# The second feed-forward matrix by seven block products in place of eight, in a float32 encoder step

## Chip, core and metric

The kernel runs on one core of a Trainium2 chip. The metric is the device time of one execution in microseconds (us), from the first to the last instruction's work; less is better. Beside the times of plain runs there is one profiled execution, whose trace gives every instruction's start and duration. TensorE multiplies, VectorE and ScalarE work elementwise, GpSimd (POOL) does little here, SyncE (SP) issues the loads of weights.

## What is computed

One layer of an encoder for 512 prompt tokens and 64 sample tokens (T = 576), width 1024, all in float32. The part that is touched is the last third, the feed-forward with its residual, and the final norm:

```python
hn = rmsnorm(x, norm2_g[l]) * (1 + sc2) + sh2
x = x + gt2 * (jnp.square(jax.nn.relu(hn @ w_ff1[l])) @ w_ff2[l])
...
y = rmsnorm(x, final_norm_g) * (1 + scf) + shf
```

w_ff1 is 1024 x 4096 and w_ff2 4096 x 1024. Everything before (norms, projections, a convolution, a gated delta rule) is the same in both kernels.

## The kernel before

**Tiles.** x and all activations lie with features on partitions: 8 feature tiles of 128 by 576 tokens. A weight tile is 8 blocks of 128 x 128 (all 1024 inputs for 128 outputs, 512 KB). The program has 160 such tiles in a row, N_FF = 96 is the first of the feed-forward's 64. Every float32 product is made of three products of a rounded high part and a low part: w_hi by f_hi, w_hi by f_lo, w_lo by f_hi (line 617). With 8 blocks, three products and two halves of 288 tokens (HALF), a tile is 48 matmuls of 288 columns into two PSUM banks; tiles alternate between two pairs of banks of gp.

**How a tile is made ready.** SP loads tile n + 4 into one of four places of w_raw once tile n is split (load, line 309). ScalarE rounds it (w_hi, two places, w_split, line 1096), VectorE subtracts (w_lo, lo_split, line 1496). Both do tile n + 2 right behind the copy of tile n out of PSUM (evac, line 1250), so that a tile is ready well ahead.

**Feed-forward.** The hidden 4096 features go in four quarters, q = 0 to 3, of 1024. ff1(q) makes 8 tiles of relu(.)^2 (VectorE line 1945, f_hi line 1418, f_lo line 1948) in one of two buffers. ff2(q) takes those 8 as inputs and adds the result of each output tile, times the gate, onto xT (add_residual, line 1953). The order is ff1(0), then ff1(q + 1) and ff2(q) for q = 0, 1, 2, then ff2(3). TensorE goes from one to the next without a wait for f, since a whole ff1 lies between.

**The end.** In ff2(3) each finished tile of xT is squared, scaled and transposed to token order between the products (to_tokens, line 1021). The last tile is made in two parts of 384 and 192 tokens (last_products, line 1057), and the sum of squares of the first part, its root and the first rows of y are made while TensorE works on the second. The orders on all engines are written out by hand; counters (semaphores such as tile_done, w_lo_done, bank_free) tie them together. Each engine works through its own list in order, so an instruction that waits holds up all behind it.

## Time and profile before

| | us |
|---|---|
| median of 3 runs | 1243.01 |
| lowest, highest | 1242.7, 1244.49 |
| span of the profiled execution, first to last instruction | 1241.9 |
| TensorE busy (PE) | 1220.0, 98% |
| VectorE busy (DVE) | 659.3, 53% |
| ScalarE busy (ACT) | 441.4, 36% |
| feed-forward, first product to end of the span | 813.8 to 1241.9 |
| last ff2 (q = 3), start | 1175.45 |

The profile gives busy time by engine, groups of instructions by line, the chain that ended last, and the timeline of any stretch. In its rows PE is TensorE, DVE VectorE, ACT ScalarE; a trailing q means the engine's sequencer, such as SPq for DMA issues. Durations of matmuls overlap, so the pace of TensorE is read from starts.

### The profile page before, as it was taken

What the parts mean: (1) busy time and instruction counts of PE and PEld (TensorE: products, weight loads), DVE (VectorE), ACT (ScalarE), POOL (GpSimd) and SP (SyncE); (2) the same over time, 40 slices, a digit from 0 to 9 for tenths busy, and PEclk for the clock granted to TensorE, in tenths of its full rate; (3) what the DMA queues carried; (4) which work ended last, traced back from release to release, by engine and by line L of the source; (5) the groups of instructions that cost most, each with busy time, mean ns of one, the idle gap of its engine ahead of it and who ended that gap; (6) DMA issues with size and microseconds to landing.
All of it is one profiled execution on the core that took longest, in us unless ns stands there. A gap on an engine that the chain in (4) does not pass through costs nothing.

```text
span 1241.9 us, 27254 instructions
## 1 busy us (share of the span) xinstructions
PE 1220.0 (98%) x11471; PEld 1167.6 (94%) x11471; DVE 659.3 (53%) x920; ACT 441.4 (36%) x792; POOL 121.0 (10%) x281
## 2 busy tenths in 40 slices
PE   6999999999999999999999999999999999999997
PEld 3899999999999999989999999979999999999997
DVE  5675666445464454535968984463443343343334
ACT  4584443122232221315243333363332332232254
POOL 4011112102012021021100001000200000000000
PEclk8999999999999999999999999999999999999999
DMA  9732323212222122235855557413422222322212
GB/s 330 237 82 72 86 71 93 65 49 70 78 69 61 53 69 57 58 89 181 245 169 145 168 205 303 121 52 85 136 77 77 84 84 85 85 85 75 81 52 77
DMA packets 181566, 135.44 MB, mean 109 GB/s; under 512 B 4554, under 2 KB 168876, under 8 KB 180184
## 3 DMA queue, kind: packets, MB, share of 16 engines
q1 hardware_dynamic: 174228, 105.36, 29.3%
q0 software_dynamic: 6976, 28.48, 6.8%
q8 instruction: 80, 1.31, 0.4%
q14 instruction: 22, 0.18, 0.0%
q10 hardware_dynamic: 260, 0.10, 0.0%
HBM read 128.02 MB, written 5.90 MB: 108 GB/s over the span
## 4 chain that ended last, share of the span: by engine, by line
PE 95%; DVE 2%; DMA 1%; ACT 1%; SPq 1%; issue 0%; POOL 0%; DVEq 0%; ACTq 0%
PE gp L617 81%; PE dp L847 2%; PE dp L857 1%; DMA ada_w<-in_ada_w 1%; PE gp L643 1%; PE dp L914 1%; PE dp L880 1%; PE dp L907 1%; PE dp L899 1%; PE dp L859 1%; PE dp L886 1%; PE dp L817 1%; PE dp L661 0%; SPq L317 0%; PE dp L889 0%
## 5 line engine op out<-in xcount | busy, mean ns | idle before, releaser
L617 PE MATMUL gp<-a_hi,w_hi 128*128 128x288 f32 x1888 | 414.8, 301 | 1.6 <-DVE w_lo L1496 1.6
L617 PE MATMUL gp<-a_hi,w_lo 128*128 128x288 f32 x1888 | 404.1, 296 | 0.0
L617 PE MATMUL gp<-a_lo,w_hi 128*128 128x288 f32 x1888 | 403.7, 295 | 0.0
L617 PEld LDWEIGHTS gp<-a_hi,w_hi 128*128 128x128 f32 x1888 | 302.1, 189 | 13.8 <-issue 6.1
L617 PEld LDWEIGHTS gp<-a_hi,w_lo 128*128 128x128 f32 x1888 | 303.9, 189 | 0.0
L617 PEld LDWEIGHTS gp<-a_lo,w_hi 128*128 128x128 f32 x1888 | 303.7, 189 | 0.0
L1496 DVE TENSOR_TENSOR w_lo<-w_raw,w_hi 128x1024 fp32r<-128x1024 f32 x160 | 198.0, 1238 | 110.2 <-ACT w_hi L1096 109.3
L1250 ACT ACTIVATE xp<-gp 128x576 f32<-128x576 f32 x113 | 73.7, 652 | 455.2 <-PE gp L617 435.1
L1096 ACT ACTIVATE w_hi<-w_raw 128x1024 fp32r<-128x1024 f32 x160 | 168.7, 1054 | 0.0
L617 PE MATMUL gp<-f_hi,w_hi 128*128 128x288 f32 x496 | 106.7, 297 | 0.0
L617 PE MATMUL gp<-f_hi,w_lo 128*128 128x288 f32 x496 | 106.3, 296 | 0.0
L617 PE MATMUL gp<-f_lo,w_hi 128*128 128x288 f32 x496 | 106.2, 296 | 0.0
L1953 DVE SCALAR_TENSOR_TENSOR xT<-xp,mod,xT 128x512 f32 (+3 forms) x62 | 29.4, 516 | 123.4 <-ACT xp L1250 123.4
L1945 DVE SCALAR_TENSOR_TENSOR acc<-xp 128x576 f32<-128x576 f32 x32 | 24.3, 758 | 109.8 <-ACT xp L1250 109.8
L617 PEld LDWEIGHTS gp<-f_hi,w_lo 128*128 128x128 f32 x496 | 79.9, 189 | 0.0
L617 PEld LDWEIGHTS gp<-f_lo,w_hi 128*128 128x128 f32 x496 | 79.9, 189 | 0.0
L617 PEld LDWEIGHTS gp<-f_hi,w_hi 128*128 128x128 f32 x496 | 79.8, 189 | 0.0
L1857 DVE SCALAR_TENSOR_TENSOR ada_sum<-ada_half,c_act,ada_sum 128x1024 f32<-128x1024 f32 x56 | 68.7, 1280 | 0.0
L1629 DVE SCALAR_TENSOR_TENSOR acc<-xp,vecs,acc 128x579 f32<-128x579 f32 x72 | 59.2, 822 | 7.1 <-DVE acc L1627 1.2
L1715 DVE TENSOR_TENSOR mm<-mm,dp 128x256 f32<-128x256 f32 (+1 forms) x45 | 15.9, 391 | 74.6 <-PE dp L859 74.6
L518 POOL TENSOR_TENSOR nb<-at,lvl 128x512 f32<-128x512 f32 (+1 forms) x30 | 35.5, 1189 | 73.7 <-PE dp L847 51.9
L1260 ACT ACTIVATE p<-dp 128x256 f32<-128x256 f32 (+1 forms) x25 | 9.2, 367 | 91.0 <-PE dp L847 91.0
(322 smaller groups left out, 1206.5 us busy)
## 6 DMA issues: line engine op xcount, KB each, us to landing
w_raw<-in_w_in SPq DMA_DIRECT2D x72, 512.0 KB, 3.8
w_raw<-in_w_ff SPq DMA_DIRECT2D x64, 512.0 KB, 4.0
ada_half<-in_ada_w POOLq DMA_DIRECT2D x32, 512.0 KB, 4.6
ada_w<-in_ada_w SPq DMA_DIRECT2D x16, 512.0 KB, 9.8
w_raw<-in_w_a_out SPq DMA_DIRECT2D x8, 512.0 KB, 4.2
w_raw<-in_w_b_out SPq DMA_DIRECT2D x8, 512.0 KB, 3.9
w_raw<-in_w_o SPq DMA_DIRECT2D x8, 512.0 KB, 6.2
fin_vu<-in_final_ada_w POOLq DMA_DIRECT2D x4, 1024.0 KB, 18.0
```

What stands on the lines that cost most here:

```text
L518: pool.tensor_tensor(nb[:, l % 2, 0:n].rearrange("p c h i -> p (c h) i"), at_[:, 0:n].rearrange("p c h i -> p (c h) i"), m, ALU.mult).then ...
L617: last = T_.matmul(gp[:, 2 * b + h, 0:HALF], wp[:, b, k, :], ap[:, k, h * HALF:(h + 1) * HALF], start=(k == 0 and wp is w_hi and ap is hi) ...
L643: last = T_.matmul(gp[:, 2 * b + h, 0:HALF], wp[:, b, k, :], ap[:, k, h * HALF:(h + 1) * HALF], start=(k == 0 and wp is w_hi and ap is hi) ...
L847: last = T_.matmul(cols(B3[o, at * CH:(at + 1) * CH], l, 0), nb[b, l % 2, e, hp, :], cols(mm[b, 0, e, hp, :], l, 0), start=True, stop=True)
L1096: AC(w_hi[:, j % 2, :, :], w_raw[:, j, :, :], ACT.Copy).then_inc(S["w_hi_done"], 1)
L1250: AC(halves(out), bank(b), func, scale=scale).then_inc(S["bank_free"], 1)
L1496: TT(w_lo[:, j % 2, :, :], w_raw[:, j, :, :], w_hi[:, j % 2, :, :].bitcast(F32), ALU.subtract)\
L1629: ins = STT(acc[:, b, 0:W], xp[:, b, tap:tap + W], cw[:, tap, ds(n, 1)], acc[:, b, 0:W], ALU.mult, ALU.add)
L1715: last = TT(m, m, cols(dp[:, 2 + t, 0:n * HP * CH], l, t), ALU.add)
L1857: STT(out, w, c_act[:, k, g:g + 1], out, ALU.mult, ALU.add).then_inc(S["ada_added"], 1)
L1945: STT(acc[:, b, 0:T], xp[:, b, 0:T], 0.0, xp[:, b, 0:T], ALU.max, ALU.mult).then_inc(S["tmp_free"], 1)
L1953: last = STT(xT[:, t, c], xp[:, b, c], mod_c(t, g), xT[:, t, c], ALU.mult, ALU.add)
```

## The change

The second matrix is applied in pairs: two output tiles (256 features) by eight input tiles, taken as a 2 x 2 arrangement of weight blocks (even and odd input tiles e, first and second output tile) against a 2 x 2 arrangement of activations (even and odd tiles, first and second half of the tokens). Such a 2 x 2 product is formed from seven block products in place of eight, with sums of blocks on both sides. A block product is four 128 x 128 blocks by 288 tokens, three times: 12 matmuls. There are 16 such pairs (q = 0 to 3, m = 0 to 3).

- **Weights.** The seven are called w11, w12, w22 (plain blocks) and s1 to s4 (sums). SP loads per pair one whole tile, the block w21 twice (once for s1, once into w_s3) and w22. VectorE forms s1 = w21 + w22, s2 = s1 + w11, s4 = s2 + w12 in place, and s3 = w21 + w11 (add_weights, line 2219). Each block product has its own w_hi (hi_of, line 1627) and w_lo (lo_of, line 2204) of 512 columns, in rings of four half places.
- **Activations.** For two hidden tiles f has seven halves (f_hi, f_lo): three as they are, four as differences (f_sum, lines 2232 to 2240), 1152 columns in two of the steps. There are five such sets.
- **Order.** In place of ff1 and ff2 there are "up" pairs (two tiles of w_ff1, 96 matmuls) and "down" pairs. Four down pairs stand in a run; before the run of q = 0, 1, 2 goes the first up pair of q + 1, behind it the other three. The run of q = 3 follows its last up pair at once.
- **Results.** PSUM banks hold running sums from which others are taken: ScalarE copies a bank to keep1, keep2 or keep5 (keep, lines 1656 and 1661), VectorE subtracts that from another bank (the mixes, lines 2267, 2272, 2277; each counts mixed_in) and adds the result to xT (lines 2254, 2290). The last product of a pair is read from PSUM. The product s1 of the next pair stands between s2 and s3 and is written to the bank that the first mix (keep1) reads; it waits for it.
- **The end.** xT's last two feature tiles are finished together. Squares are summed on VectorE over pairs of tiles; last_products and its two parts are gone.
- The loops over tiles are written out. In the diff ITEMS is the list of all products in order, issued(k) gives those whose place in the ring of halves comes free with product k.

```diff
+def ff_plan():
+    pairs = [("up", 0, u) for u in range(4)]
+    for q in range(4):
+        if q < 3:
+            pairs.append(("up", q + 1, 0))
+        pairs += [("down", q, m) for m in range(4)]
+        if q < 3:
+            pairs += [("up", q + 1, u) for u in range(1, 4)]
+    items, at = [], 0
+    for p, (kind, q, i) in enumerate(pairs):
+        if kind == "up":
+            names = [(p, "a", 2), (p, "b", 2)]
+        else:
+            names = [(p, "s1", 1)] if i == 0 else []
+            names += [(p, "w11", 1), (p, "w12", 1), (p, "s2", 1)]
+            names += [(p + 1, "s1", 1)] if i < 3 else []
+            names += [(p, "s3", 1), (p, "s4", 1), (p, "w22", 1)]
+        for name in names:
+            items.append(name + (at,))
+            at += name[2]
+    return pairs, items
...
+        def load_first(p):
...
+                sp.wait_ge(S["w_lo_done"], split_items(p - 2, "a" if PAIRS[p - 2][0] == "up" else "s4"))
+            sp.dma_start(w_raw[:, 2 * (p % 2), :, :], w_block(p, "w1")).then_inc(first_full[p % 2], 16)
+        def load_second(p):
...
+            sp.wait_ge(S["w_lo_done"], split_items(p - 2, "b" if PAIRS[p - 2][0] == "up" else "s4"))
+            sp.dma_start(raw_block(p, "s1"), w_block(p, "w21")).then_inc(sum_full[p % 2], 16)
+            if PAIRS[p - 2][0] == "down":
+                sp.wait_ge(S["w_lo_done"], split_items(p - 2, "w22"))
+            sp.dma_start(raw_block(p, "w22"), w_block(p, "w22")).then_inc(second_full[p % 2], 16)
+        def load_s3(p):
+            if p > DOWN[0]:
+                sp.wait_ge(S["w_lo_done"], split_items(DOWN[DOWN.index(p) - 1], "s3"))
+            sp.dma_start(w_s3[:, :, :], w_block(p, "w21")).then_inc(s3_full, 16)
+        for p in range(1, len(PAIRS)):
+            load_first(p)
+            if PAIRS[p - 1][0] == "down":
+                load_s3(p - 1)
+            load_second(p)
+        load_s3(len(PAIRS) - 1)
...
+        def down(p, name, units=range(4)):
+            q, i = PAIRS[p][1:]
+            d = downs(p)
+            z, y, x = i % 2, 1 - i % 2, 2 + i % 2
+            bank, blk, opens = {"s1": (z, 3, True), "w11": (x, 0, True), "w12": (y, 2, True), "s2": (x, 4, False),
+                                "s3": (x, 5, False), "s4": (z, 1, False), "w22": (x, 6, False)}[name]
+            if 0 in units:
+                pe.wait_ge(S["w_lo_done"], split_items(p, name))
+                if name == "s1" and i == 0:
+                    pe.wait_ge(S["bank_free"], N_FF + 2 * ups(p) - 2 + 3)
+                elif name == "s1":
+                    pe.wait_ge(S["mixed_in"], 3 * (d - 1) + 1)
+                elif name == "w11" and i < 2:
+                    pe.wait_ge(S["bank_free"], N_FF + 2 * ups(p) - 1 + 3)
+                elif name == "w11":
+                    pe.wait_ge(S["x_new"], 4 * (d - 1))
+                elif name == "w12" and i:
+                    pe.wait_ge(S["mixed_in"], 3 * (d - 1) + 3)
+                elif name == "s2":
+                    pe.wait_ge(S["kept_out"], kept(p, "keep1"))
+                elif name == "s3":
+                    pe.wait_ge(S["kept_out"], kept(p, "keep2"))
+                elif name == "s4":
+                    pe.wait_ge(S["kept_out"], kept(p, "keep5"))
+                elif name == "w22":
+                    pe.wait_ge(S["mixed_in"], 3 * d + 2)
+            for u in units:
+                if i == 0:
+                    pe.wait_ge(S["f_split"], 4 * q + u + 1)
+                f = (4 * q + u) % FW
+                s0 = (END[p, name] - 1) % 4
+                for wp, ap in ((w_hi, f_hi), (w_hi, f_lo), (w_lo, f_hi)):
+                    last = T_.matmul(gp[:, bank, 0:HALF], wp[:, s0 // 2, 4 * (s0 % 2) + u, :], ap[f][:, blk, :],
+                                     start=(opens and u == 0 and wp is w_hi and ap is f_hi), stop=(u == 3 and wp is w_lo),
+                                     skip_group_check=True)
+            if 3 in units:
+                last.then_inc(S["slot_done"], 1)
...
+        def hi_of(k):
+            p, name, width, at = ITEMS[k]
...
+                act.wait_ge(S["slot_done"], at + width - 4)
+            if name in ("a", "w11", "w12"):
+                act.wait_ge(first_full[p % 2], ADA_IN + 16 * loads_before(p, "first"))
+            elif name in ("b", "w22"):
+                act.wait_ge(second_full[p % 2], ADA_IN + 16 * loads_before(p, "second"))
+            else:
+                act.wait_ge(S["w_summed"], summed(p, name))
+            AC(slots(w_hi, k), raw_block(p, name), ACT.Copy).then_inc(S["w_hi_done"], 1)
+        def keep(p, name):
+            i, d = PAIRS[p][2], downs(p)
+            z, x = i % 2, 2 + i % 2
+            if name == "keep5":
+                act.wait_ge(S["slot_done"], END[p, "s1"])
+                if d >= 2:
+                    act.wait_ge(S["x_new"], 4 * (d - 2) + 2)
+                AC(keep5[d % 2][:, :], gp[:, z, 0:HALF], ACT.Copy).then_inc(S["kept_out"], 1)
+            else:
+                act.wait_ge(S["slot_done"], END[p, "w11" if name == "keep1" else "s2"])
+                if d:
+                    act.wait_ge(S["x_new"], 4 * (d - 1) + (1 if name == "keep1" else 3))
+                AC((keep1 if name == "keep1" else keep2)[:, :], gp[:, x, 0:HALF], ACT.Copy).then_inc(S["kept_out"], 1)
...
-        def ff2(q, n0):
-            with dve.Fori(0, 2) as i:
-                for j in range(4):
-                    n, b, t = n0 + 4 * i + j, j % 2, 4 * i + j
-                    dve.wait_ge(S["bank_free"], n + 1 + 2)
-                    add_residual(t, b).then_inc(S["tmp_free"], 1)
-                    lo_split(n + 2, (j + 2) % 4)
+        def lo_of(k):
+            p, name = ITEMS[k][:2]
+            dve.wait_ge(S["w_hi_done"], N_FF + k + 1)
+            TT(slots(w_lo, k), raw_block(p, name), slots(w_hi, k).bitcast(F32), ALU.subtract).then_inc(S["w_lo_done"], 1)
+        def add_weights(k):
+            p, name = ITEMS[k][:2]
+            other = {"s1": "w22", "s2": "w11", "s3": "w11", "s4": "w12"}[name]
+            if name == "s1":
+                dve.wait_ge(sum_full[p % 2], ADA_IN + 16 * loads_before(p, "sum"))
+                dve.wait_ge(second_full[p % 2], ADA_IN + 16 * loads_before(p, "second"))
+            else:
+                dve.wait_ge(first_full[p % 2], ADA_IN + 16 * loads_before(p, "first"))
+            if name == "s3":
+                dve.wait_ge(s3_full, ADA_IN + 16 * loads_before(p, "s3"))
+            elif name != "s1":
+                dve.wait_ge(S["w_lo_done"], split_items(p, "s1" if name == "s2" else "s2"))
+            TT(raw_block(p, name), raw_block(p, name), raw_block(p, other), ALU.add).then_inc(S["w_summed"], 1)
+        def up_step(p, tile, ks):
+            n, j = N_FF + 2 * ups(p) + tile, ups(p)
+            hi, lo = f_hi[j % FW], f_lo[j % FW]
+            even, odd = [(acc[:, e, HALF:T], acc[:, e, 0:HALF]) for e in range(2)]
+            dve.wait_ge(S["bank_free"], n + 1 + 2)
+            STT(acc[:, tile, 0:T], xp[:, tile, 0:T], 0.0, xp[:, tile, 0:T], ALU.max, ALU.mult).then_inc(S["tmp_free"], 1)
+            for k in ks:
+                lo_of(k)
+            dve.wait_ge(S["tmp_free"], n - N_WA + 3)
+            if tile == 0:
+                TT(f_sum[:, 0, :], even[0], even[1], ALU.subtract).then_inc(S["f_summed"], 1)
+                dve.wait_ge(S["f_hi_done"], 3 * j + 1)
+                STT(lo[:, 0, :], acc[:, 0, HALF:T], -1.0, hi[:, 0, :].bitcast(F32), ALU.mult, ALU.subtract)
+                return
+            dve.wait_ge(S["f_summed"], 2 * j + 1)
+            ch.note(TT(f_sum[:, 1, :], odd[1], f_sum[:, 0, :], ALU.add))
+            TT(f_sum[:, 2, :], even[1], odd[1], ALU.subtract)
+            ch.wait()
+            TT(f_sum[:, 3, :], odd[0], f_sum[:, 1, :], ALU.subtract).then_inc(S["f_summed"], 1)
+            dve.wait_ge(S["f_hi_done"], 3 * j + 2)
+            TT(lo[:, 1:3, :], acc[:, 1, 0:T].rearrange("p (h c) -> p h c", h=2), hi[:, 1:3, :].bitcast(F32), ALU.subtract)
+            dve.wait_ge(S["f_hi_done"], 3 * j + 3)
+            TT(lo[:, 3:7, :], f_sum[:, :, :], hi[:, 3:7, :].bitcast(F32), ALU.subtract).then_inc(S["f_split"], 1)
...
+        def down_step(p, name, ks):
+            q, i = PAIRS[p][1:]
+            d, t = downs(p), 2 * i
+            z, y, x = i % 2, 1 - i % 2, 2 + i % 2
+            if name == "w12":
+                dve.wait_ge(S["slot_done"], END[p, "w12"])
+                dve.wait_ge(S["kept_out"], kept(p, "keep1"))
+                TT(keep1[:, :], gp[:, y, 0:HALF], keep1[:, :], ALU.subtract).then_inc(S["mixed_in"], 1)
+                after = (t, LATE, keep1, HALF, 4 * d)
+            elif name == "s3":
+                dve.wait_ge(S["slot_done"], END[p, "s3"])
+                dve.wait_ge(S["kept_out"], kept(p, "keep5"))
+                TT(keep5[d % 2][:, :], gp[:, x, 0:HALF], keep5[d % 2][:, :], ALU.subtract).then_inc(S["mixed_in"], 1)
+                after = (t + 1, EARLY, keep5[d % 2], 0, 4 * d + 1)
+            elif name == "s4":
+                dve.wait_ge(S["slot_done"], END[p, "s4"])
+                dve.wait_ge(S["kept_out"], kept(p, "keep2"))
+                TT(keep2[:, :], gp[:, z, 0:HALF], keep2[:, :], ALU.subtract).then_inc(S["mixed_in"], 1)
+                after = (t, EARLY, keep2, 0, 4 * d + 2)
+            for k in ks:
+                lo_of(k)
+            if name in ("w12", "s3", "s4"):
+                dve.wait_ge(S["mixed_in"], 3 * d + {"w12": 1, "s3": 2, "s4": 3}[name])
+                onto_x(*after).then_inc(S["x_new"], 1)
+            elif name == "w22":
+                dve.wait_ge(S["slot_done"], END[p, "w22"])
+                j = 4 * d + 3
+                if j >= 16:
+                    dve.wait_ge(S["x_new"], j - 15)
+                for g, c in LATE:
+                    last = STT(xT[:, t + 1, c], gp[:, x, c.start - HALF:c.stop - HALF], mod[:, 2, t + 1 + KT:t + 2 + KT, g],
+                               xT[:, t + 1, c], ALU.mult, ALU.add)
+                last.then_inc(S["x_new"], 1)
...
+                down_step(p, name, issued(k))
+                if q == 3 and i and name == "s2":
+                    sum_squares(i - 1)
+            for m in (issued(k + 1) if k + 1 < len(ITEMS) else ()):
+                if ITEMS[m][1][0] == "s":
+                    add_weights(m)
```

**How the orders move.** The first place is VectorE in the middle of a run of second-matrix work. Before, for each output tile, from the start of a loop over ff2's tiles:

```order
L1953 ISA [waits bank_free]
L1953 ISA
L1953 SCALAR_TENSOR_TENSOR xT<-xp,mod,xT 128x512
L1953 ISA
L1953 SCALAR_TENSOR_TENSOR xT<-xp,mod,xT 128x64
L1496 TENSOR_TENSOR w_lo<-w_raw,w_hi 128x1024 [waits w_hi_done]
L1963 REGISTER_ALU
```

Now, in a pair in the middle of a run, from the sum s2 to the first mix (keep_143 is keep1, keep_144 keep2, w_s_142 is w_s3):

```order
L2219 TENSOR_TENSOR w_raw<-w_raw 128x512 [waits w_lo_done,ada_full1]
L2277 TENSOR_TENSOR keep_144<-gp,keep_144 128x288 [waits kept_out,slot_done]
L2204 TENSOR_TENSOR w_lo<-w_raw,w_hi 128x512 [waits w_hi_done]
L2254 SCALAR_TENSOR_TENSOR xT<-keep_144,mod,xT 128x288 [waits x_new,mixed_in]
L2219 TENSOR_TENSOR w_raw<-w_raw 128x512 [waits ada_full2,ada_full4]
L2204 TENSOR_TENSOR w_lo<-w_raw,w_hi 128x512 [waits w_hi_done]
L2290 SCALAR_TENSOR_TENSOR xT<-gp,mod,xT 128x224 [waits x_new,slot_done]
L2290 SCALAR_TENSOR_TENSOR xT<-gp,mod,xT 128x64
L2219 TENSOR_TENSOR w_s_142<-w_s_142,w_raw 128x512 [waits ada_full6,ada_full1]
L2204 TENSOR_TENSOR w_lo<-w_s_142,w_hi 128x512 [waits w_hi_done]
L2219 TENSOR_TENSOR w_raw<-w_raw 128x512 [waits w_lo_done,ada_full1]
L2267 TENSOR_TENSOR keep_143<-gp,keep_143 128x288 [waits kept_out,slot_done]
```

One w_lo of 1024 columns and a residual per tile have become sums, mixes, w_lo of 512 columns and residuals in turn.

The second place is VectorE where the first matrix's tile gives way to the second's. Before, the last tile of ff1(1) and the small work on the last norm's scale behind it:

```order
L1944 REGISTER_ALU
L1945 SCALAR_TENSOR_TENSOR acc<-xp 128x576 [waits bank_free]
L1496 TENSOR_TENSOR w_lo<-w_raw,w_hi 128x1024 [waits w_hi_done]
L1947 REGISTER_ALU
L1948 ISA [waits f_hi_done]
L1948 TENSOR_TENSOR f_lo<-acc,f_hi 128x576
L1941 REGISTER_ALU
L1941 COMPARE_AND_BRANCH
L1529 TENSOR_TENSOR mod<-dp,vecs 128x32 [waits ada_t]
L1535 TENSOR_SCALAR scales<-mod 128x16 [waits dve_own]
L1536 TENSOR_TENSOR scales<-scales,vecs 128x16 [waits dve_own]
```

Now, the end of the last up pair and the first steps of the run:

```order
L2204 TENSOR_TENSOR w_lo<-w_raw,w_hi 128x512 [waits w_hi_done] x2
L2237 TENSOR_TENSOR f_sum<-acc,f_sum 128x288 [waits f_summed,tmp_free]
L2238 TENSOR_TENSOR f_sum<-acc 128x288
L2240 TENSOR_TENSOR f_sum<-acc,f_sum 128x288 [waits dve_own]
L2242 TENSOR_TENSOR f_lo_138<-acc,f_hi_133 128x576 [waits f_hi_done]
L2244 TENSOR_TENSOR f_lo_138<-f_sum,f_hi_133 128x1152 [waits f_hi_done]
L2219 TENSOR_TENSOR w_raw<-w_raw 128x512 [waits ada_full2,ada_full4]
L2204 TENSOR_TENSOR w_lo<-w_raw,w_hi 128x512 [waits w_hi_done]
L2219 TENSOR_TENSOR w_s_142<-w_s_142,w_raw 128x512 [waits ada_full6,ada_full1]
L2204 TENSOR_TENSOR w_lo<-w_s_142,w_hi 128x512 [waits w_hi_done]
L2219 TENSOR_TENSOR w_raw<-w_raw 128x512 [waits w_lo_done,ada_full1]
L2267 TENSOR_TENSOR keep_143<-gp,keep_143 128x288 [waits kept_out,slot_done]
```

The low parts of f stand ahead of sum s1 of the next pair, and three sums ahead of the first mix.

The third place is ScalarE in the same kind of work. Before, from the start of the loop over ff2's tiles:

```order
L1249 REGISTER_ALU [waits tile_done]
L1250 ACTIVATE xp<-gp 128x576 [waits tmp_free]
L1095 ISA
L1096 ACTIVATE w_hi<-w_raw 128x1024 [waits w_raw_full2]
L1247 REGISTER_ALU
```

Now, from w_hi of s2 and s1 on through one pair (keep_1_146 is keep5):

```order
L1627 ACTIVATE w_hi<-w_raw 128x512 [waits w_summed,slot_done] x2
L1661 ACTIVATE keep_143<-gp 128x288 [waits x_new,slot_done]
L1627 ACTIVATE w_hi<-w_s_142 128x512 [waits w_summed,slot_done]
L1627 ACTIVATE w_hi<-w_raw 128x512 [waits w_summed,slot_done]
L1661 ACTIVATE keep_144<-gp 128x288 [waits x_new,slot_done]
L1627 ACTIVATE w_hi<-w_raw 128x512 [waits ada_full3,slot_done]
L1656 ACTIVATE keep_1_146<-gp 128x288 [waits x_new,slot_done]
L1627 ACTIVATE w_hi<-w_raw 128x512 [waits ada_full0,slot_done] x2
L1627 ACTIVATE w_hi<-w_raw 128x512 [waits w_summed,slot_done]
L1627 ACTIVATE w_hi<-w_s_142 128x512 [waits w_summed,slot_done]
```

Copies to keep1, keep2 and keep5 stand between roundings, some of which wait for VectorE's sums (w_summed).

## Rows read from the trace of the kernel before

**Rows 1.** The page: busy time by engine, and the chain by engine

```profile
PE 1220.0 (98%) x11471; PEld 1167.6 (94%) x11471; DVE 659.3 (53%) x920; ACT 441.4 (36%) x792; POOL 121.0 (10%) x281
...
PE 95%; DVE 2%; DMA 1%; ACT 1%; SPq 1%; issue 0%; POOL 0%; DVEq 0%; ACTq 0%
```

**Rows 2.** Chain that ended last, 1130 to 1242: start, us, what

```profile
1129.91 45.33 PE gp L617 x340
...
1175.45 12.78 PE gp L617 x96
1188.24 0.44 PE dp L1021 x4
```

**Rows 3.** Stretches: length, PE, PEld, DVE, ACT, POOL busy, clock, DMA share, GB/s

```profile
1087.00:1141.00 54.00, 54.00 (x407) 54.00 (x406) 22.17 (x27) 17.81 (x24) 0.00 (x0) 1.00 0.27 78
...
1175.00:1223.00 48.00, 48.00 (x368) 47.99 (x367) 18.92 (x26) 24.03 (x45) 2.20 (x4) 1.00 0.14 38
```

**Rows 4.** Timeline at a tile's end in ff2(2): start, us, engine, instruction

```profile
1130.28 0.42 PE L617 MATMUL gp<-f_hi,w_hi 128*128 128x288 f32 x2
...
1130.56 0.65 ACT L1250 ACTIVATE xp<-gp 128x576 f32<-128x576 f32 x1 [4.21 <-PE gp L617]
...
1131.11 1.05 ACT L1096 ACTIVATE w_hi<-w_raw 128x1024 fp32r<-128x1024 f32 x1
...
1132.35 1.22 DVE L1496 TENSOR_TENSOR w_lo<-w_raw,w_hi 128x1024 fp32r<-128x1024 f32 x1
```

**Rows 5.** Timeline in ff1(1)

```profile
881.08 1.05 ACT L1096 ACTIVATE w_hi<-w_raw 128x1024 fp32r<-128x1024 f32 x1
...
882.17 1.23 DVE L1496 TENSOR_TENSOR w_lo<-w_raw,w_hi 128x1024 fp32r<-128x1024 f32 x1 [0.19 <-ACT w_hi L1096]
883.31 0.75 DVE L1948 TENSOR_TENSOR f_lo<-acc,f_hi 128x576 f32 x1
```

**Rows 6.** Groups on VectorE by form: busy us, mean ns, idle before

```profile
L1945 DVE SCALAR_TENSOR_TENSOR acc<-xp 128x576 f32<-128x576 f32 x32 | 24.3, 758 | 109.8 <-ACT xp L1250 109.8
...
L1953 DVE SCALAR_TENSOR_TENSOR xT<-xp,mod,xT 128x512 f32 x24 | 18.0, 752 | 102.2 <-ACT xp L1250 102.2
...
L1953 DVE SCALAR_TENSOR_TENSOR xT<-xp,mod,xT 128x64 f32 x24 | 6.7, 279 | 0.0
...
L1725 DVE TENSOR_TENSOR kbe<-by_chunk,eg 128x512 f32<-128x512 f32 x9 | 6.1, 683 | 0.0
...
L1600 DVE TENSOR_TENSOR row<-dp,row 64x288 f32<-64x288 f32 x1 | 0.4, 443 | 0.0
```

**Rows 7.** Groups on ScalarE by form: busy us, mean ns, idle before

```profile
L1207 ACT ACTIVATE xp<-gp 128x288 f32<-128x288 f32 x24 | 9.8, 410 | 77.3 <-PE gp L617 77.3
...
L1163 ACT ACTIVATE ab_both<-ab_raw 128x512 fp32r<-128x512 f32 x1 | 0.6, 630 | 2.7 <-POOL ab_raw L469 2.7
```

**Rows 8.** SP's issues (ns), and DMA of 750 to 813: packets, MB, share; us to landing

```profile
L309 SPq DMA_DIRECT2D w_raw<-in_w_ff x64: 372/373/1251, 776.9 to 1193.1; - x64
...
q1 hardware_dynamic: 9939, 5.01, 29.2%
...
w_raw<-in_w_ff SPq DMA_DIRECT2D x6, 512.0 KB, 4.0
```

**Rows 9.** Last matmuls with w_lo (start range), and VectorE's timeline at the end

```profile
L1057 PE MATMUL gp<-f_hi,w_lo x16: 272/306/342, 1223.7 to 1232.7; 128*128 128x384 f32 x8, 128*128 128x192 f32 x8
...
1231.12 1.15 DVE L1986 SCALAR_TENSOR_TENSOR z_tok<-z_tok,rstd,shift 128x896 f32<-128x896 f32 x1 [1.86 <-ACT rstd L1468]
...
1237.30 1.27 DVE L2006 SCALAR_TENSOR_TENSOR z_smp<-z_smp,rstd,shift 64x1024 f32<-64x1024 f32 x1
```

**Rows 10.** TensorE early: timeline, and stretches with PE busy, clock, DMA share, GB/s

```profile
22.74 1.89 PE L661 MATMUL dp<-ada_w,c_act 128*2 128x512 f32 x8 [1.87 <-DMA ada_w<-in_ada_w]
...
22.00:23.00 1.00, 0.26 (x4) 0.58 1.23 243
32.00:33.00 1.00, 1.00 (x9) 0.80 1.06 389
```

470 lines of the change are left out of this document (285 added, 185 removed).

## The prediction

> **What bounds the kernel now.** I read the engines' shares and the chain first: TensorE is busy 98% of the span and carries 95% of the chain that ended last [rows 1]. The pieces of the chain in the feed-forward show it without a gap: 340 matmuls of 288 columns in 45.33 us, 96 in 12.78 us, so 0.1333 us each and 6.40 us for a tile of 48 [rows 2]. The table of stretches gives VectorE's load there: 22.2 us of 54 and, in the last ff2, 18.9 of 48, with the clock at full [rows 3]. So today a matmul taken away is time taken away, and VectorE and ScalarE have room on average. Average room isn't what decides here. The timeline shows how one tile is handed on: the next tile's first matmul starts at 1130.28, ScalarE's copy of the finished bank at 1130.56 (0.28 later), w_hi ends at 1132.16 and VectorE's w_lo starts at 1132.35 [rows 4]. In a tile that has a second step the handover from ScalarE to VectorE is only 0.04 (882.13 to 882.17) [rows 5]. A weight tile is made two tiles ahead, so all of it hides behind 6.40 us. After the change the unit is a product of 12 matmuls, 1.60 us, and the hand-overs come seven to a pair.
>
> **What goes.** 16 pairs of output tiles take 84 matmuls in place of 96: 192 x 0.1333 = 25.6 us of TensorE, all on the chain. The loops' registers go too (0.25 of idle VectorE time before x, hidden).
>
> **What comes, in rows' prices.** VectorE with two tensors: 512 columns 0.68, 576 columns 0.75, 1024 columns 1.22, 288 columns out of PSUM 0.44, a square of 576 0.76 [rows 4 to 6]. Back to back the next starts 0.09 before the end (882.17 to 883.31 for 1.23 long [rows 5]), so steps of 0.60, 0.66, 1.14 and 0.37. The residual step on 288 columns: 0.75 for 512 and 0.28 for 64 [rows 6] give 0.52, a step of 0.43; in two parts 0.56. ScalarE: 512 columns 0.63, 288 out of PSUM 0.41 [rows 7]. A pair then asks VectorE for 7 w_lo and 4 sums (11 x 0.60), 3 mixes (1.1), residuals (2 x 0.43 + 2 x 0.56): 9.7 us of work in the 11.2 us that the pair's 84 matmuls take. That would still fit; the order does not let it run through. Sums s1 and s3 are followed at once, on the same in-order queue, by the w_lo of that very sum, which needs ScalarE's w_hi of it. Sum starts at 0, w_hi at 0.72, w_lo at 1.39: 0.79 us of idle VectorE each; behind sum s2 a mix fills half of it and 0.42 stays.
>
> **The wait that the change adds.** The product s1 of the next pair is written to the bank from which keep1 is mixed, so TensorE waits there for VectorE's mix (line 2267, semaphore mixed_in), which stands at the end of a long stretch of VectorE's queue. I walk one pair in the middle of a run, from the start of s1 at 0. s3 ends at 3.20, seen at 3.48: mix of keep5 to 3.85. w_lo of w12 starts at 4.15 (its w_hi could start only at 3.48), to 4.75; residual to 5.18; sum s2 to 5.78; mix of keep2 to 6.15; w_lo of s2 not before 6.57, to 7.17; residual 7.60; sum s1 starts 7.60, its w_lo 8.99 to 9.59; residual in two parts to 10.14; sum s3 starts 10.14, its w_lo 11.53 to 12.13; sum s4 to 12.73; mix of keep1 12.73 to 13.18; TensorE starts the next s1 at 13.24. A pair thus takes 13.24 us; its matmuls take 11.2 and before it took 12.80. The point from which this decides: from "s3 seen" to "mix done" the queue takes 9.70 us, and it may take 7.66 (11.2 less 3.20, 0.28 and 0.06).
>
> **A whole run of four pairs** (q = 0 to 2), from the end of the last up tile. VectorE first finishes that tile: copy out to 0.93, square 0.96 to 1.64, two w_lo to 2.84, three differences to 3.92, low parts to 4.59, and the 1152-wide one, after ScalarE's copy of 1.15 (its prices for 512 and 1024 columns carried on), to 6.52. Only then sum s1 (w_lo to 8.51), sum s3 (w_lo to 10.50), sum s4 to 11.10, mix to 11.55. TensorE has 6.4 us of work by then and starts s1 of the second pair at 11.6: 5.2 us idle. It also waits for keep1 in between, since ScalarE has w_hi of s1 queued ahead of that copy (s2 starts at 8.2 for 4.8). Two full cycles follow, 26.5. Then s1, s3, s4, w22 are 6.4, and the last pair has no s1 between s2 and s3, so s3 waits for keep2, queued behind two w_hi: 1.2 idle, 10.8 in all. Sum 11.6 + 26.5 + 6.4 + 10.8 = 55.3 against 8 x 6.40 = 51.2: **+4.1 a run, +12.3 for three**. The 6.4 us of matmuls saved in a run come back as 10.5 of waiting. The up tiles between runs ask VectorE for 7.5 us per 12.8 (two w_lo 2.3, two squares 1.4, four differences 1.5, low parts 2.4): nothing changes there.
>
> **The last run** (q = 3) follows straight on up tiles whose f it needs, +0.4. Five additions of squares (0.66 each, about half of them in the waiting queue), ScalarE's squares, scalings and z copies ahead of w_hi and keep copies, and 30 transposes at 0.11 [rows 2] make its two full cycles about 14.3 and its end 20.3: 12.0 + 28.6 + 20.3 = 60.9. Behind it, both parts of the square sums wait for the last product, where now the first y row starts at 1231.12, ahead of the last matmul with w_lo at 1232.7 [rows 9]. From it 1.4 us of sums and roots to the first y, 6.1 for the y rows, 3.3 from the last y to the end as now [rows 9]: I take 10.8. 71.7 against 1241.9 - 1175.45 = 66.5 [rows 2]: **+5.2**.
>
> **Loads.** SP now issues four loads a pair (1.25 MB for 1.0), each 0.37 us to issue [rows 8]. They leave together once s4 is split, at 0.9 of the walk. 5.01 MB took 29.2% of 63 us, 272 GB/s, and a lone 512 KB load lands after 4.0, so 2.1 is fixed [rows 8]. Then 1.25 MB land by 0.9 + 2.1 + 4.8 = 7.8, and sum s1 wants the last of them at 7.60. I take 0; 1 us a pair is the upper bound, at most 7 in all. Below zero is excluded: a load can't make the queue shorter.
>
> **Sum.** 1241.9 + 12.3 + 5.2 = 1259.4 in the profiled execution. The median of the runs lies 1.1 above its span, so **1260.5**, +1.4%. The steps' prices are good to some 3%: eight waiting cycles of 13.2 give 3 us, four run starts 1 each.
>
> A page is weighed here. The trace has the next VectorE instruction start 0.09 before the end of the one ahead [rows 5]. The Trainium skill, "VectorE: DVE Perf Modes", section "The DRAIN you can't avoid", says that the next one doesn't start until the pipe is empty. By that each of some ten back-to-back steps of a cycle would cost 0.09 more, about 9 us over the kernel, and the sum would be near 1269. The trace disagrees for this kernel's instructions, so the row is used; 1269 lies within the forecast's own range.
>
> **Rivals.**
> *VectorE keeps up (faster).* If the sums ran early enough, or w_hi were there when w_lo asks, the mix would be done before s2 ends and only 192 matmuls would count: 1243.0 - 25.6 + 1.5 for the tail = 1219; with the run starts' 5.2 left over four times, 1240. It speaks for it that VectorE's work, 9.7, is under 11.2; against it that its idle 0.79, 0.79 and 0.42 a pair follow from the order, and that s3, whose end starts the walk, can't be earlier. It would need 2 us less in the queue of each pair. 0.13.
> *No change.* The same, half way: a queue 0.5 us shorter in each of eight cycles and starts 1.5 shorter give 1250; to come within 0.2% it takes half as much again, and the stretch of such prices is narrow. 0.03.
> *The clock falls (slower still).* The granted clock fell to half (1.2 GHz) at 22 us, in a stretch in which TensorE waited for loads, the last time for 1.87 us, and was back ten us later [rows 10]. At each run start the change leaves TensorE idle for 5.2 of 6.8 us. If it falls there, the two products that the queue waits for (s1 and s3) take 3.2 each: up to 3.2 a run, 13 in all, 1273. With late loads beside it, 1280. No other stretch of this trace has such a gap with dense matmuls behind it. 0.16.
> The Trainium skill, "TensorE: Matmul & The Clock Gate", section "HAM oscillation — how this bites in real kernels", says that waits which break up the matmuls put the array back to half rate each time. By that rule the time would be this rival's upper end; the trace has one fall behind such waits, and here no run shows it yet in dense matmuls.
> *It doesn't do what it says.* TensorE's new order holds 12 matmuls a product and seven products a pair, so this is out.
>
> **Chances and range.** The forecast, 1248 to 1273, has 0.68; beyond it to 1278 lies half of the clock and load case. That leaves the faster rival and the far end of the slow one outside, some 2 in 10. The range is 1248 to 1278. About 0.2% is what a measurement of this kernel can tell from no change. Faster 0.13, same 0.03, slower 0.84.
>
> **What would show it.** Right: TensorE's busy time some 25 us lower in a longer span; idle time of TensorE put down to VectorE's mixes (line 2267), twelve times, three of them in each run, near 5 us at the starts and 2 us after; starts of s1 about 13.2 us apart; VectorE idle 0.8 us before the w_lo of sums, put down to ScalarE. Wrong: s1 starts 11.2 apart and no wait for mixes; loads named as releaser of the sums; half clock in the runs.

## The result, and the profile after

The changed kernel takes **1274.2 us** (median of 4 executions, 1273.19 to 1275.0), the kernel before 1243.45 beside it (4 executions, 1242.7 to 1244.49): a ratio of 1.0247, 95% interval 1.0232 to 1.0261. It is 30.8 us slower; I had forecast 17.5. The profiled execution has a span of 1271.5 for 1241.9. In what follows a run is the four down pairs of one q, and a cycle is the time from the first matmul of one pair's product s1 to that of the next.

The page of the kernel after: busy time by engine, the chain by engine, and the two groups of the new products and roundings that answer to [rows 1] and [rows 6]:

```profile
PE 1208.5 (95%) x11304; PEld 1149.6 (90%) x11304; DVE 797.9 (63%) x1222; ACT 481.7 (38%) x894; POOL 123.0 (10%) x283
...
PE 81%; DVE 7%; ACT 4%; issue 4%; SPq 2%; DMA 2%; DVEq 0%; POOL 0%; ACTq 0%
...
L1210 PE MATMUL gp<-f_hi,w_hi 128*128 128x288 f32 x448 | 138.3, 309 | 39.9 <-DVE keep L2267 19.6
...
L2204 DVE TENSOR_TENSOR w_lo<-w_raw,w_hi 128x512 fp32r<-128x512 f32 (+1 forms) x126 | 102.4, 818 | 42.7 <-ACT w_hi L1627 42.5
```

TensorE's chain has gone from 95% to 81% of the span: the time is in waits. What TensorE waited for from 820 to 1272, and VectorE in one cycle from s1 to s1 (905.47 to 919.11):

```profile
PE gp L1210 <- DVE keep L2267: 19.6, 12, 2.2
PE gp L1210 <- issue: 10.6, 4, 3.4
PE gp L1210 <- ACT keep L1661: 6.8, 7, 1.3
PE gp L1210 <- DVE f_lo L2244: 2.8, 1, 2.8
...
DVE w_lo L2204 <- ACT w_hi L1627: 3.2, 6, 0.8
```

Twelve waits for the first mix, as forecast, and behind them waits for ScalarE's copies and at the starts of runs ("issue" is a wait whose releaser the profile doesn't name; at 888.35 it ends with ScalarE's copy to keep1). VectorE is idle 3.2 us in a cycle, all of it put down to w_hi. 2.3 of that are holes behind its own sums (0.76, 0.76, 0.39 and 0.39). The other 0.9 stands behind ScalarE, which itself waits for TensorE there: 0.73 behind the copy to keep5, 0.21 behind a rounding.

The starts of the runs are not quite as forecast. The long wait there is the one ahead of s2, 3.3 to 3.4 us in the first three runs, and it ends with the copy to keep1; the wait for the mix that follows is 0.4 to 1.7.

The four runs of down pairs, from the end of the last up tile to the last product, by stretches (us, PE, PEld, DVE, ACT, POOL busy, granted clock, DMA share, GB/s), and then the tail:

```profile
880.09:936.82 56.73, 47.36 (x338) 45.95 (x337) 42.70 (x81) 22.85 (x43) 0.00 (x0) 0.97 0.33 89
986.82:1045.62 58.80, 47.61 (x338) 46.12 (x337) 42.71 (x81) 22.89 (x43) 0.00 (x0) 0.97 0.30 85
1096.89:1158.19 61.30, 49.99 (x338) 48.44 (x337) 42.75 (x81) 22.89 (x43) 0.00 (x0) 0.92 0.30 82
1196.78:1257.38 60.60, 51.93 (x369) 49.27 (x367) 45.67 (x85) 33.77 (x67) 6.39 (x8) 0.97 0.18 50
1257.40:1271.50 14.10, 5.54 (x81) 4.41 (x80) 7.22 (x9) 3.51 (x12) 0.00 (x0) 0.71 0.46 169
```

I had 55.3 for each of the first three, 60.9 and 10.8. VectorE's work is the same 42.7 in the first three though their lengths differ by 4.6: those runs differ in clock and in loads, not in work. In the third the clock is 0.92. A stretch of it:

```profile
1107.00:1108.00 1.00, 0.49 (x3) 0.14 (x1) 1.00 (x2) 0.00 (x0) 0.00 (x0) 0.50 0.00 0
1110.00:1111.00 1.00, 1.00 (x6) 1.00 (x6) 0.74 (x2) 0.00 (x0) 0.00 (x0) 0.50 0.14 42
1115.00:1116.00 1.00, 1.00 (x9) 1.00 (x8) 1.00 (x3) 0.00 (x0) 0.00 (x0) 1.00 0.31 77
```

At 0.50 (1.2 GHz) matmuls start 0.24 us apart, for 0.1333 [rows 2]. It fell 1.1 us after TensorE had resumed from an idle 3.32 and was back at 1113.1.

**One cycle in full**, the timeline of VectorE with the starts of s1 on TensorE (start, us, engine, operation, idle before):

```profile
905.47 0.37 PE L1210 MATMUL gp<-f_hi,w_hi 128*128 128x288 f32 x1 [2.15 <-DVE keep L2267]
...
908.92 0.46 DVE L2272 TENSOR_TENSOR keep<-gp,keep 128x288 f32<-128x288 f32 x1
909.58 0.69 DVE L2204 TENSOR_TENSOR w_lo<-w_raw,w_hi 128x512 fp32r<-128x512 f32 x1 [0.21 <-ACT w_hi L1627]
...
912.07 0.69 DVE L2204 TENSOR_TENSOR w_lo<-w_raw,w_hi 128x512 fp32r<-128x512 f32 x1 [0.39 <-ACT w_hi L1627]
912.68 0.51 DVE L2254 SCALAR_TENSOR_TENSOR xT<-keep,mod,xT 128x288 f32<-128x288 f32 x1
913.26 0.69 DVE L2219 TENSOR_TENSOR w_raw<-w_raw 128x512 f32<-128x512 f32 x1
914.71 0.69 DVE L2204 TENSOR_TENSOR w_lo<-w_raw,w_hi 128x512 fp32r<-128x512 f32 x1 [0.76 <-ACT w_hi L1627]
...
915.87 0.68 DVE L2219 TENSOR_TENSOR w_s<-w_s,w_raw 128x512 f32<-128x512 f32 x1
917.30 0.69 DVE L2204 TENSOR_TENSOR w_lo<-w_s,w_hi 128x512 fp32r<-128x512 f32 x1 [0.76 <-ACT w_hi L1627]
...
918.52 0.45 DVE L2267 TENSOR_TENSOR keep<-gp,keep 128x288 f32<-128x288 f32 x1
919.11 0.37 PE L1210 MATMUL gp<-f_hi,w_hi 128*128 128x288 f32 x1 [2.13 <-DVE keep L2267]
```

The walk of the prediction can be laid beside it, counted from s1: mix of keep5 3.48, here 3.45; w_lo of w12 4.15 and 4.11; w_lo of s2 6.57 and 6.60; sum s1 7.60 and 7.79; sum s3 10.14 and 10.40; first mix 12.73 and 13.05; next s1 13.24 and 13.64. The holes of 0.76 and 0.39 stand where it had 0.79 and 0.42.

### The profile page after: what moved, and what is told of

The parts are those of the page before. It is cut to its first block, busy times and chain, and to the rows that moved or that the text cites. A ratio compares the mean times of both kernels' runs of the same rounds, so it can differ in the third digit from the quotient of the medians.

```text
span 1271.5 us, 26974 instructions
## 1 busy us (share of the span) xinstructions
PE 1208.5 (95%) x11304; PEld 1149.6 (90%) x11304; DVE 797.9 (63%) x1222; ACT 481.7 (38%) x894; POOL 123.0 (10%) x283
## 4 chain that ended last, share of the span: by engine, by line
PE 81%; DVE 7%; ACT 4%; issue 4%; SPq 2%; DMA 2%; DVEq 0%; POOL 0%; ACTq 0%
PE gp L766 48%; PE gp L1172 15%; PE gp L1210 6%; ACT w_hi L1627 3%; PE dp L996 2%; DVE w_raw L2219 2%; SPq L433 1%; PE dp L1006 1%; PE gp L792 1%; DMA ada_w<-in_ada_w 1%; DVE w_s L2219 1%; PE dp L1063 1%; PE dp L1029 1%; DMA w_raw<-in_w_ff 1%; PE dp L1056 1%
## 5 line engine op out<-in xcount | busy, mean ns | idle before, releaser
L766 PEld LDWEIGHTS gp<-a_hi,w_hi 128*128 128x128 f32 x1408 | 224.7, 189 | 11.6 <-issue 6.9
L766 PEld LDWEIGHTS gp<-a_hi,w_lo 128*128 128x128 f32 x1408 | 226.4, 188 | 0.0
L1755 DVE TENSOR_TENSOR w_lo<-w_raw,w_hi 128x1024 fp32r<-128x1024 f32 x98 | 120.2, 1227 | 100.9 <-ACT w_hi L1300 100.1
L1210 PE MATMUL gp<-f_hi,w_hi 128*128 128x288 f32 x448 | 138.3, 309 | 39.9 <-DVE keep L2267 19.6
L1210 PE MATMUL gp<-f_lo,w_hi 128*128 128x288 f32 x448 | 135.7, 303 | 0.0
L1210 PE MATMUL gp<-f_hi,w_lo 128*128 128x288 f32 x448 | 135.7, 303 | 0.0
L2204 DVE TENSOR_TENSOR w_lo<-w_raw,w_hi 128x512 fp32r<-128x512 f32 (+1 forms) x126 | 102.4, 818 | 42.7 <-ACT w_hi L1627 42.5
L1210 PEld LDWEIGHTS gp<-f_hi,w_hi 128*128 128x128 f32 x448 | 87.7, 196 | 45.8 <-issue 36.6
L1627 ACT ACTIVATE w_hi<-w_raw 128x512 fp32r<-128x512 f32 (+1 forms) x126 | 90.4, 729 | 89.8 <-DVE w_raw L2219 64.6
L1454 ACT ACTIVATE xp<-gp 128x576 f32<-128x576 f32 x50 | 32.5, 651 | 191.9 <-PE gp L766 175.3
L1300 ACT ACTIVATE w_hi<-w_raw 128x1024 fp32r<-128x1024 f32 x98 | 103.4, 1056 | 0.5 <-DMA w_raw<-in_w_in 0.5
```

The costliest lines, as they stand in the source:

```text
L766: last = T_.matmul(gp[:, 2 * b + h, 0:HALF], wp[:, b, k, :], ap[:, k, h * HALF:(h + 1) * HALF], start=(k == 0 and wp is w_hi and ap is hi) ...
L1210: last = T_.matmul(gp[:, bank, 0:HALF], wp[:, s0 // 2, 4 * (s0 % 2) + u, :], ap[f][:, blk, :], start=(opens and u == 0 and wp is w_hi and ...
L1300: AC(w_hi[:, j % 2, :, :], w_raw[:, j, :, :], ACT.Copy).then_inc(S["w_hi_done"], 1)
L1454: AC(halves(out), bank(b), func, scale=scale).then_inc(S["bank_free"], 1)
L1627: AC(slots(w_hi, k), raw_block(p, name), ACT.Copy).then_inc(S["w_hi_done"], 1)
L1755: TT(w_lo[:, j % 2, :, :], w_raw[:, j, :, :], w_hi[:, j % 2, :, :].bitcast(F32), ALU.subtract)\
```

## Experiments

The theory at this point: VectorE's queue, with the holes that its sums make, is the pace of a pair, and the run starts are its second half. Rivals: the loads, the clock, ScalarE's order. The table gives for every kernel the median (of four executions; five for "filled holes, loads", two for "no sums") and, from its profiled execution, the length of the four runs of down pairs, from the first product's start to the last one's end; without any wait a run of the first three would be 28 x 1.60 = 44.8.

| kernel | us | ratio to before | run 0, 1, 2, 3 |
|---|---|---|---|
| after | 1274.2 | 1.0247 | 56.6, 58.7, 61.2, 60.7 |
| no sums | 1235.5 | 0.9933 | 47.4, 47.5, 47.4, 54.1 |
| mix moved | 1275.8 | 1.0259 | 57.5, 57.0, 57.2, 64.2 |
| filled waits | 1272.4 | 1.0228 | 57.2, 56.9, 57.9, 61.7 |
| w_s3 loaded last | 1274.5 | 1.0255 | 58.3, 57.7, 58.1, 62.0 |
| filled holes | 1256.4 | 1.0101 | 53.9, 53.0, 54.7, 58.1 |
| mix moved, copies first | 1272.8 | 1.0238 | 57.8, 56.2, 56.7, 63.9 |
| filled holes, early start | 1256.0 | 1.0105 | 49.3, 50.4, 52.1, 58.1 |
| sums on GpSimd | 1263.9 | 1.0169 | 58.5, 52.9, 53.2, 60.9 |
| filled holes, loads | 1248.5 | 1.0038 | 50.8, 50.9, 50.8, 58.2 |
| all of these | 1234.4 | 0.9924 | 45.6, 45.8, 45.7, 59.0 |
| all, copies first | 1238.0 | 0.9953 | 47.4, 47.4, 47.3, 58.8 |

### The sums left out

```diff
                 if ITEMS[m][1][0] == "s":
-                    add_weights(m)
+                    pass
```

ScalarE waits for the loads instead of the sums; the products then use weight blocks that were never added.

> The four weight sums of a pair are left out (ScalarE rounds the raw block as soon as it is loaded); everything else, all 84 matmuls of a pair too, stays. Theory (TensorE waits for the first mix, which stands at the end of a queue of sums, each with a w_lo behind it that waits for ScalarE): without sums the queue from the end of s3 to the mix is 6.9 us by the same prices, under the 7.66 allowed, so the waits for the mix at line 2267 vanish, s1 starts come 11.2 us apart, only a rest of some 2 us at each run start stays: 1228 to 1236 us. Rival (the loss is clock and late loads, or the low parts of f): TensorE still waits, 1255 or more.

Measured: 1235.48, inside the theory's range (ratio 0.9933, 0.9913 to 0.9953). No down product waits for a mix in it, cycles are 11.0 to 11.2, and the first three runs are 47.4 long with the clock at 1.00. The four sums of a pair cost about 39 us, together with the holes behind them and the falls of the clock behind the waits that they make. That is more than the 25.6 that the missing eighth product saves.

### The first mix moved ahead of two sums

In this and the following kernels VectorE's steps are first listed in the order of the kernel after, and then single ones are moved.

```diff
+        for p in DOWN:
+            if PAIRS[p][2] < 3:
+                move(("mix", p, "w12"), before=("add", NTH[p, "s3"]))
```

> Only the place of the first mix (keep1) in VectorE's order is changed: it goes ahead of the sum s3, its w_lo and the sum s4 that stood before it. VectorE's work is the same to the instruction. Theory: the mix is done about when s2 ends, so that wait goes; then VectorE's whole list bounds, 9.7 us of work and 2.8 of waits for ScalarE (s4's w_lo now waits too): 12.5 us a pair in place of 13.6, and run starts of 9.0 in place of 11.75. 4 x 2.7 + 8 x 1.1 = 20 us less: 1254, with the clock's part up to 5 less: 1249 to 1256. Rival (VectorE has simply too much work, order is no matter): 1270 to 1275.

Measured: 1275.79, 1.0259 (1.0241 to 1.0276). My theory said 1249 to 1256, so it was wrong as it stood: TensorE no longer waits for the mix, and the time is the same. TensorE's waits, and VectorE's in the cycle from 1011.33 to 1025.43, which is 14.1 long:

```profile
PE gp L1210 <- ACT keep L1661: 25.6, 19, 2.6
...
DVE w_lo L2204 <- ACT w_hi L1627: 49.8, 91, 1.5
DVE w_raw L2219 <- DMA w_raw<-in_w_ff: 6.8, 6, 1.7
...
1013.88 0.69 DVE L2204 TENSOR_TENSOR w_lo<-w_s,w_hi 128x512 fp32r<-128x512 f32 x1 [0.76 <-ACT w_hi L1627]
1014.49 0.69 DVE L2219 TENSOR_TENSOR w_raw<-w_raw 128x512 f32<-128x512 f32 x1
1015.93 0.69 DVE L2204 TENSOR_TENSOR w_lo<-w_raw,w_hi 128x512 fp32r<-128x512 f32 x1 [0.76 <-ACT w_hi L1627]
...
1023.57 0.69 DVE L2219 TENSOR_TENSOR w_raw<-w_raw 128x512 f32<-128x512 f32 x1 [1.11 <-DMA w_raw<-in_w_ff]
```

The wait has changed its name: TensorE now waits for ScalarE's copies, which stand behind w_hi of s1 and of s4, and these wait for VectorE's sums. VectorE never waits for TensorE in this cycle. Its idle is 0.76 three times, 0.39, and 1.11 for a load, 3.8 in all, and 10.3 of work beside it makes the 14.1. The mix had filled the hole between sum s4 and its w_lo (0.39 was left); moved, it opens that hole to 0.76. Beside the cycle of the kernel after, the 0.9 of idle behind TensorE is gone, and 0.4 of hole and 1.1 of load have come in its place. My theory had counted 9.7 of work, where 10.3 are measured (it took the steps ahead of the holes without their last 0.09), and no load.

The loads are thus part of the answer. Six of VectorE's sums wait for a load here, 6.8 us in all, where two did in the kernel after (2.0). How much the moved mix would have gained with loads in another order was not measured. Two readings are left: VectorE's queue closes on itself whatever TensorE waits for by name (A), or ScalarE's order is the cause (B). Both are tried below.

### Matmuls put into the waits

```diff
+                if q in (1, 2):
+                    for _ in range(24 if name == "s2" and i == 0 else 12 if name == "s1" and i else 6 if name == "s3" and i == 3 else 0):
+                        T_.matmul(dp[:, 0, 0:HALF], a_hi[:, 0, 0:P], a_hi[:, 0, 0:HALF], start=True, stop=True)
                 pe.wait_ge(S["w_lo_done"], split_items(p, name))
```

> Matmuls on a_hi into an unused bank are put into TensorE's waits in the runs of q = 1 and 2: 24 ahead of s2 of the first pair, 12 ahead of every s1 that waits, 6 ahead of s3 of the last pair; their results are used by nothing. Theory that the half clock seen in these two runs costs time by itself: the three falls at 1027, 1106 and 1140 us go, their 1.9 + 1.6 + 1.6 us come back, 1268 to 1271. Rival (slow matmuls hid in waits anyway, the cost was none): 1273 to 1276.

Measured: 1272.36, ratio 1.0228 (1.0211 to 1.0245), between the theory's 1268 to 1271 and the rival's 1273 to 1276. Runs 1 and 2, by stretches:

```profile
989.04:1046.10 57.06, 54.97 (x405) 53.37 (x403) 42.75 (x81) 22.92 (x43) 0.00 (x0) 1.00 0.32 88
1097.35:1155.40 58.05, 54.95 (x405) 53.36 (x403) 42.76 (x81) 22.94 (x43) 0.00 (x0) 1.00 0.31 87
```

The clock is at full in both, and they are 1.8 and 3.3 shorter than in the kernel after: some 5 us for the clock in those two executions. In the median only 1.8 of it can be seen, and the profiled spans differ by 1.3, since runs 0 and 3, which have no such matmuls, are 1.5 longer together, and what lies between and behind the runs is 2.2 longer. Where the clock falls differs from trace to trace: the last run, with the same work in both kernels, has one fall in the kernel after and two here. The clock is a small term; its size is between 1.8 and 5 us.

### The w_s3 block loaded last

```diff
             load_first(p)
+            load_second(p)
             if PAIRS[p - 1][0] == "down":
                 load_s3(p - 1)
-            load_second(p)
```

> SP issues w21 and w22 for a pair's s1 ahead of the block w_s3 for the pair before it, no other change. Theory: the two waits of VectorE for loads (0.7 and 1.3 us, runs of q = 1 and 2) go, since w22 lands 0.25 MB earlier: 1271 to 1273. Rival (load order moves the wait to the sum s3, or noise): 1273 to 1276.

Measured: 1274.5, ratio 1.0255 (1.0238 to 1.0272): no gain that can be told, as the rival said. In the trace cycles without a disturbance are 13.48, and sum s1 stands at 7.62 after s1, where the walk had 7.60. The kernel after has one such cycle, the first of run 1, 13.49 long. In three of its eight cycles (13.61 to 13.64), the shown one among them, the sum starts some 0.15 late, which fits a load that ends just too late; the profile names none. The two late loads that it does name (2.0 us) became others; the waits for loads in this trace:

```profile
DVE w_raw L2219 <- DMA w_raw<-in_w_ff: 1.0, 1, 1.0
DVE w_s L2219 <- DMA w_s<-in_w_ff: 1.0, 2, 0.6
```

### A against B: the holes filled

```diff
+        for p in DOWN:
+            i = PAIRS[p][2]
+            if i < 3:
+                move(("mix", p, "w12"), before=("add", NTH[p, "s3"]))
+                move(("add", NTH[p, "s4"]), after=("add", NTH[p, "s3"]))
+                move(("residual", p, "w12"), after=("lo", NTH[p, "s3"]))
+                move(("residual", p, "s3"), after=("add", NTH[p + 1, "s2"]))
+            if i < 2:
+                move(("residual", p, "w22"), before=("lo", NTH[p + 2, "s1"]))
```

> Steps of VectorE in another order, the same work: for the first three pairs of a run the first mix stands ahead of sum s3 (as in the run with the mix alone moved), sum s4 stands straight behind sum s3 (ahead of w_lo of s3), the residual of w12 behind w_lo of s3, the residual of s3 behind sum s2, the residual of w22 ahead of w_lo of s1. So each gap of 0.76 us between a sum and its own w_lo has a step in it. Theory A, formed after the run with the mix alone moved: VectorE's queue is itself the period of a pair (10.2 us of steps, 3.2 to 3.4 us of waits for ScalarE's w_hi and up to 1.1 for a load in 14.1), and in the run with the mix alone the mix had merely left a gap open that it had filled. With the gaps filled a pair takes 11.2 to 12.8 (12.8 if the load of the next w21 block then ends the wait for sum s1), the kernel 1245 to 1260. Rival B: what holds TensorE is ScalarE's order, copies to keep1 and keep2 that stand behind roundings of sums; that order is not touched here, so no gain over the run with the mix alone: 1270 to 1277.

Measured: 1256.38, ratio 1.0101 (1.0082 to 1.0121), so A's range, 17.8 under the kernel after and 19.4 under the one with the mix alone, with no step removed and ScalarE's order untouched. VectorE's waits for w_hi are 19.4 lower too (30.4 for 49.8), and its waits for loads rise from 6.8 to 11.4. The waits, then the w_lo of a sum and the next sum s1:

```profile
DVE w_lo L2204 <- ACT w_hi L1627: 30.4, 78, 2.2
DVE w_raw L2219 <- DMA w_raw<-in_w_ff: 9.0, 7, 2.2
...
1009.38 0.69 DVE L2204 TENSOR_TENSOR w_lo<-w_s,w_hi 128x512 fp32r<-128x512 f32 x1 [0.16 <-ACT w_hi L1627]
...
1018.26 0.69 DVE L2219 TENSOR_TENSOR w_raw<-w_raw 128x512 f32<-128x512 f32 x1 [2.10 <-DMA w_raw<-in_w_ff]
```

### A against B: ScalarE's copies first

```diff
+            inner = [NTH[r + 1, "s1"] for r in DOWN if PAIRS[r][1] < 3 and PAIRS[r][2] < 3]
+            inner += [NTH[r, "s4"] for r in DOWN if PAIRS[r][1] < 3 and PAIRS[r][2] < 3]
+            if q < 3 and i < 3 and name in ("w11", "s2"):
+                hi_of(NTH[p + 1, "s1"] if name == "w11" else NTH[p, "s4"])
             for m in issued(k):
-                hi_of(m)
+                if m not in inner:
+                    hi_of(m)
```

> The first mix ahead of sum s3, as in the run with the mix alone moved, and on ScalarE, for q < 3 and the first three pairs, the copy to keep1 ahead of w_hi of the next s1 and the copy to keep2 ahead of w_hi of s4. Theory A (VectorE's queue with its gaps is the period): the waits put down to the keep copies (19 of them, 25.6 us) move elsewhere, cycles stay at 13.1 to 14.3, and only the start and end of a run gain some 1 us: 1270 to 1275. Rival B (ScalarE's order holds TensorE): most of the waits for keep go, cycles near 12, the kernel 1250 to 1260.

Measured: 1272.84, ratio 1.0238 (1.0217 to 1.0258), as A said. TensorE's waits for copies go from 25.6 to 11.2 and waits for mixes take their place:

```profile
PE gp L1210 <- DVE keep L2271: 13.5, 14, 2.2
PE gp L1210 <- ACT keep L1661: 11.2, 9, 2.7
PE gp L1210 <- issue: 3.7, 6, 0.9
```

B falls as the main cause. Copies and mixes together are 24.7 for 25.6: for these only the name moved. The waits that the profile calls "issue", mostly at the run starts, did fall, from 10.7 to 3.7 us, and the time by 2.9: ScalarE's order is worth about that much here, not the 20 of rival B.

### The start of a run brought forward

To the filled order, with the w_s3 block loaded last as above:

```diff
+        for p in DOWN:
+            q, i = PAIRS[p][1:]
+            if i == 0:
+                move(("up", p - 1, 1, "differences"), after=("add", NTH[p + 1, "s1"]))
+                if q < 3:
+                    move(("up", p - 1, 1, "low"), after=("residual", p + 3, "s3"))
+                else:
+                    move(("up", p - 1, 1, "low"), after=("up", p - 1, 1, "differences"))
```

ScalarE's wide copy goes behind keep1 of the first pair for q < 3.

> The order of the filled run, and with it: the load of the w_s3 block issued behind the pair's other loads, and at the start of a run the differences of f behind sum s1's place in the queue and, for q < 3, ScalarE's copy of the 1152 columns and VectorE's low part of them put off until the last up tile is needed at the next down run. Theory A: loads no longer end the wait for sum s1, cycles 11.2 to 12, starts 2 us shorter: 1232 to 1246, so faster than the kernel before or equal to it. Rival: if loads or the falling clock bound the filled run, this one is at most 3 us better than it.

Measured: 1255.98, ratio 1.0105 (1.0088 to 1.0122): the theory's 1232 to 1246 is missed and the rival holds, 0.4 better than the filled order. The runs are 9.8 shorter together, but VectorE's waits for loads have grown from 11.4 to 16.7, and TensorE now waits in up tiles:

```profile
DVE w_raw L2226 <- DMA w_raw<-in_w_ff: 8.5, 7, 1.5
DVE w_s L2226 <- DMA w_s<-in_w_ff: 8.2, 3, 3.5
...
PE gp L1172 <- DVE keep L2273: 6.2, 3, 2.1
```

VectorE's sums come 11.9 apart, and the loads are what ends last in that: sum s1 at 1009.95 waits 1.20 for a block that SP issued at 1004.80. And the low part of 1152 columns, put ahead of the last mix of a run, makes the next up tile wait 2.1 us each time. That was my placing.

### The sums on GpSimd

```diff
-                if ITEMS[m][1][0] == "s":
+                if ITEMS[m][1][0] == "s" and PAIRS[ITEMS[m][0]][1] in (0, 3):
                     add_weights(m)
```

For q = 1 and 2 the same function, with GpSimd's addition, stands in GpSimd's list.

> In runs q = 1 and 2 the weight sums are made on GpSimd in place of VectorE; runs 0 and 3 as before. GpSimd's sum of 512 columns took 1.30 us (its row of 24 such steps in the same kernel). Theory A: VectorE's steps of a pair fall from 10.2 to 7.8, the waits for w_hi shift to sums 0.6 later; cycles in runs 1 and 2 are 11.2 to 12, the kernel 1260 to 1268. Rival C: the two engines hold each other up, as the w_lo of 1024 columns that took 3.15 us in place of 1.22 at 888.49 of the kernel before, while GpSimd added the shift: each of the four sums then costs VectorE some 1.3 us, cycles stay at 13.5 or get longer: 1273 to 1285.

Measured: 1263.94, ratio 1.0169 (1.0152 to 1.0186), in the theory's range: runs 1 and 2 are 5.7 and 7.9 shorter than in the kernel after, and run 0 is not. But the theory's cycles of 11.2 to 12 did not come. They are 12.8 and 13.4 in run 1, 13.1 and 13.9 in run 2, near the 13.5 of rival C; in the kernel after they were 13.5, 14.3, 15.5 and 14.8. The rest of the gain lies in starts that are 1.9 and 2.4 shorter and in ends that are 2.2 and 2.3 shorter. In part it is the clock, which was at half for 3.4 us in these two runs and for 13.7 in the kernel after. That the time fell into the theory's range is thus partly luck. GpSimd is no free place. The groups of w_lo of plain blocks and of s3, in run 1, and GpSimd's sums:

```profile
L2224 DVE TENSOR_TENSOR w_lo<-w_raw,w_hi 128x512 fp32r<-128x512 f32 x22 | 17.9, 816 | 8.9 <-ACT w_hi L1647 8.6
L2224 DVE TENSOR_TENSOR w_lo<-w_s,w_hi 128x512 fp32r<-128x512 f32 x4 | 4.2, 1044 | 2.1 <-ACT w_hi L1647 2.1
...
L749 POOL TENSOR_TENSOR w_raw<-w_raw 128x512 f32<-128x512 f32 x24 | 36.2, 1517 | 215.3 <-DMA w_raw<-in_w_ff 175.7 <-DVE w_lo L2224 39.6
```

In the same stretch of the kernel after these w_lo take 690 and 692 ns. Beside a sum of GpSimd one takes up to 1.40, and two sums of GpSimd took 3.44 for 2 x 1.30: part of what moves away comes back on both engines.

### The loads in the order in which they are wanted

On the filled order; in the middle and at the end of a run:

```diff
+            if PAIRS[p - 1][0] == "down" and PAIRS[p - 2][0] == "down":
+                load_s3(p - 1)
+                if PAIRS[p][0] == "down":
+                    load_second(p)
+                    load_first(p)
+                else:
+                    load_first(p)
+                    load_second(p)
+                continue
```

> The filled order and another order of loads: for each pair in the middle or at the end of a run, w_s3 of the pair before first (its buffer is free first), then the w21 and w22 blocks, whose sum is wanted first, and w11 with w12 last. In the filled run TensorE still waited 12.5 us for copies to keep1 and keep2, which stood behind roundings of sums that had waited for loads (9.0 and 2.4 us, ten times, up to 2.2). Theory: the load is now what ends last in a filled pair; with this order most of the 11.4 us of waits for loads go and three quarters of them show in the time: 1246 to 1251. Rival: once the sums are not late, ScalarE's order gives the same waits: 1254 to 1258.

Measured: 1248.55, ratio 1.0038 (1.0024 to 1.0052), as expected. VectorE's waits for loads fall from 11.4 us to one of 0.3:

```profile
DVE w_raw L2228 <- DMA w_raw<-in_w_ff: 0.3, 1, 0.3
```

In runs 0 to 2 TensorE now has two waits each that the profile names, 3.4 at the start and 0.8 near the end. In the middle nothing waits, and the second cycle of each run takes 11.1 to 11.2. Behind each wait at the start the clock was at half for 3.4 us.

### All of it

The early start once more, with the wide low part behind the last residual of the run:

```diff
-                    move(("up", p - 1, 1, "low"), after=("residual", p + 3, "s3"))
+                    move(("up", p - 1, 1, "low"), after=("residual", p + 3, "w22"))
```

> The filled order, the load order of the run before this one, and the earlier start of a run: sum s1 ahead of the differences of f, and for q < 3 the wide low part of f put off behind the residual of the last w22 of the run (in the run with the earlier start it stood ahead of the last mix, which the next up tile waited for: 2.1 us, three times). Theory: the kernel 1236 to 1246, faster than the kernel before or the same. Rival: the clock, which falls to half after the gaps that remain, takes the gain back: 1246 to 1252.

Measured: **1234.38**, ratio 0.9924 (0.9908 to 0.9941): 39.8 us under the kernel after and 0.8% faster than the kernel before; 14.2 under the one without the early start, or 4.7 a run, and below the 1236 to 1246 that I expected. In the two profiled executions a run is 5.1 shorter: the wait of 3.4 at its start is gone and with it the fall of the clock, which stays at full in all three. The 3.4 us at half that stood there before cost an estimated 1.5, at 0.24 us a matmul for 0.133. TensorE's waits in the down products:

```profile
PE gp L1219 <- ACT keep L1675: 5.2, 6, 1.1
PE gp L1219 <- DVE f_lo L2261: 3.5, 1, 3.5
```

Runs 0 to 2 are 45.7 against 44.8. What is left is the last run (59.0, with 3.5 for f at its start), the tail, and the clock.

### And the copies first

The kernel with everything moved, with the ScalarE edit of above.

> The kernel with everything moved, and on ScalarE, for q < 3 and three pairs of four, keep1 ahead of w_hi of the next s1 and keep2 ahead of w_hi of s4. Theory: with the sums no longer late the copies hardly wait behind roundings: within 3 us of the kernel with everything moved. Rival: the waits for copies that are left (16 us in the earlier try) are ScalarE's order after all: 4 to 10 us better than it.

Measured: 1237.99, 3.6 slower: neither theory nor rival, though nearer the theory. VectorE's waits for w_hi rise from 24.3 to 31.9 us, which fits w_hi of s1 and s4 coming late behind copies that wait for a product. TensorE has three new waits of 1.0 for a mix, one at the start of each of the first three runs.

## Why the prediction was right, and where it was off

Its direction, its cause and its range held; the forecast of 1260.5 was 13.7 too low. 12.1 of that is the span, taken apart below. The other 1.6 is that the median now lies 2.7 above the profiled span, where I had carried 1.1 over. Point by point:

- **What goes.** I had named some 25 us less of TensorE's busy time as a sign; it fell by 11.5, from 1220.0 to 1208.5. Busy time isn't a count of matmuls: under the lower clock they stand 0.24 apart, and each of the many restarts counts to its end. The kernel without the sums, 8 us under the one before, shows that the products left out do give time back.
- **The steps' prices** held: w_lo and sums 0.69 and 0.68, residual 0.51, mixes 0.45, holes 0.76 and 0.39.
- **The wait that the change adds** came where forecast (line 2267), twelve times; at the run starts most of the idle time stood one product earlier, ahead of s2, which the prediction named only beside it. A full cycle: 13.24 forecast, 13.64 measured. 0.15 of the 0.40 fits a load that ends just too late, which I had taken at 0 with the landing at 7.8 and the need at 7.60; the sum started at 7.79. Three of the eight cycles have it. The rest is hand-overs, 0.06 more from each sum to the end of its w_lo and 0.08 more from the mix to TensorE.
- **The run.** 55.3 forecast; 56.7, 58.8 and 61.3 measured, 10.9 over in the three, where the span is over by 12.1. In the first run the one fall of the clock slows s2, and most of that goes into the wait behind it; so this run shows the mis-sized term of the steps: 11.75 to the second s1 for 11.6, cycles 13.63 and 13.64, the end 17.7 for 17.2. That is 1.4 a run. Beyond it runs 1 and 2 lost 6.7: some 5 is the clock by the profiled execution with filled waits (the medians show 1.8), and 2.0 are the two late loads. The clock was a rival in the prediction, with up to 13 us; it held in part beside the forecast, not in place of it.
- **The last run.** 60.9 forecast, 60.6 measured, but by other parts: its cycles were 13.61 and 14.12 for 14.3.
- **The tail.** 10.8 forecast, 14.1 measured. The rows at the end, which answer to [rows 9]:

```profile
1259.27 2.82 DVE L2322 SCALAR_TENSOR_TENSOR z_tok<-z_tok,rstd,shift 128x768 f32<-128x768 f32 x3 [1.14 <-ACT rstd L1725]
1262.45 1.02 DVE L2322 SCALAR_TENSOR_TENSOR z_tok<-z_tok,rstd,shift 128x768 f32<-128x768 f32 x1 [0.36 <-ACT rstd L1725]
1265.25 1.68 DVE L2322 SCALAR_TENSOR_TENSOR z_tok<-z_tok,rstd,shift 128x256 f32<-128x256 f32 x2 [1.77 <-ACT z_smp L1743]
1266.84 1.27 DVE L2337 SCALAR_TENSOR_TENSOR z_smp<-z_smp,rstd,shift 64x1024 f32<-64x1024 f32 x1
```

  The first y row starts 1.9 after the last product for 1.4, and the y rows take 8.8 for 6.1, with 2.1 of waiting in them: 1.77 for the second part's copy, whose transposes run with the clock at half. I had added the y rows up as if nothing could stand between them. Over the terms that leaves some 2 us less than forecast in the up tiles and before them, which I didn't trace.
- **Rivals.** "VectorE keeps up" was rightly held possible but not in this order: it needed the holes filled, the loads in another order, and the starts moved, and then gave 1234 against the 1219 to 1240 worked out for it. What the prediction didn't see is how closed the circle is. It named a wait of TensorE for a mix and the point from which it decides. Moving that mix gained nothing. The 0.9 that VectorE had stood behind TensorE went, and a hole 0.4 wider and a load of 1.1 came, so VectorE's 10.3 of work, its holes and the loads that its steps release made the same pace under another name.
- **The page on VectorE.** In the cycle shown w_lo starts at 912.07 and lasts 0.69, and the residual starts at 912.68, 0.08 before its end, though the residual has nothing to wait for. The Trainium skill, "VectorE: DVE Perf Modes", section "The DRAIN you can't avoid", says in one sentence that the next operation doesn't start until the pipe is empty, and in another that one which isn't held starts earlier. The prediction weighed the first alone; the rows of both kernels fit the second. That 1269 lay nearer the result is chance, since its cause isn't in the rows.
- **The page on the clock.** The clock fell five times in the runs, each time within or within 2 us after an idle of 2.2 to 3.4 us, and it stayed at full where matmuls filled the waits. That agrees with the Trainium skill, "TensorE: Matmul & The Clock Gate", section "HAM oscillation — how this bites in real kernels", in kind. It does not in number, where the section has a fall behind every wait of its kernel: of the four long waits at the run starts three had a fall in or behind them, and of the twelve for the mix two.

## What to carry to other kernels

A wait is named after the last link, not after the cause: moving the mix changed the name of some 26 us of waiting and hardly its length. Before a step is moved, add up the in-order queue that stands behind the wait, with its own round trips to another engine; if its work and holes make up the period, filling the holes shortens it, as far as the loads keep up. And each bound that is lifted shows the next: here holes (17.8 us), then the order of loads (7.9), then the start of a run (14.2), of which the last gave 0.4 when it was first tried, with late loads and with a step placed so that it cost 6.2 of its own.

## What the runs showed of the hardware

- GpSimd and VectorE hold each other up on elementwise steps in SBUF: w_lo of 512 columns took 690 ns alone and up to 1.40 us beside GpSimd's additions (those of s3 1044 ns in the mean), and two additions of GpSimd in a row took 3.44 for 2.60.
- Under the lower clock a matmul of 288 columns started every 0.24 us for 0.133, and in the kernel after that lasted 3 to 7 us at a time. Which of several waits of the same length has such a fall behind it differs from trace to trace, and no run here shows why.
- A sum on VectorE, ScalarE's rounding of it and VectorE's start on the result is a round trip of 1.45 us from start to start, of which 0.76 is idle on VectorE.
